# Split weights of the 512-token stretches placed 32, 96 and 160 bytes further in their buffers

## The reference, cut to what matters

```
for layer in (0, 1):
    h, hc = (a + 0.5*g*swiglu(prenorm(a)) for a in (h, hc))   # ffn1: 1024 -> 2*2816 -> 1024
    zl, zc = prenorm(h) @ w_in, prenorm(hc) @ w_in            # "even" mixer, then "odd" mixer
    h = h + gm * (mixer(zl, zc) @ mix_w_out)
    h = h + 0.5*g2*swiglu(prenorm(h))                         # ffn2; hc too, in layer 0 only
```

## Time and profile before

| what | value |
|---|---|
| median of three runs | 2996.09 us |
| the profiled execution | 2992.23 us, span 2990.5 us |
| mean granted TensorE clock | 0.996 of full speed |
| PE busy | 2932.5 us, 98% of the span, 20172 matmuls |
| PEld busy | 2580.5 us, 86% |
| DVE, ACT busy | 57%, 44% |
| DMA | 439.36 MB, 147 GB/s on average |

### The profile page before, as it was taken

The page is one execution under the profiler, slowest core; times in us unless marked ns, Lnnn a source line. Parts: engine busy times, 40 slices in busy tenths (PEclk is TensorE's granted clock), DMA queues, the critical chain, the costliest instruction groups (busy, mean ns, idle before and its releaser), DMA issues.

```text
span 2990.5 us, 52037 instructions
## 1 busy us (share of the span) xinstructions
PE 2932.5 (98%) x20172; PEld 2580.5 (86%) x20172; DVE 1690.7 (57%) x2664; ACT 1314.1 (44%) x1952; POOL 0.2 (0%) x4
## 2 busy tenths in 40 slices
PE   9999999999999999999998999999999999999999
PEld 6778878787777878888888999999899999988998
DVE  4333363545332453334666667677776776777766
ACT  4322343423222342223335656555555555556555
POOL 0000000000000000000000000000000000000000
PEclk9999999999999999999999999999999999999999
DMA  9555343146566433332322666455446654554564
GB/s 275 181 176 148 89 154 93 43 149 176 166 202 181 141 113 95 95 105 76 121 85 79 190 184 186 132 156 170 141 141 196 175 156 146 166 164 139 163 191 137
DMA packets 639011, 439.36 MB, mean 147 GB/s; under 512 B 22172, under 2 KB 627192, under 8 KB 638712
## 3 DMA queue, kind: packets, MB, share of 16 engines
q1 hardware_dynamic: 637844, 436.70, 49.1%
q10 hardware_dynamic: 996, 0.23, 0.0%
HBM read 430.84 MB, written 1.05 MB: 144 GB/s over the span
## 4 chain that ended last, share of the span: by engine, by line
PE 87%; DVE 8%; ACT 1%; issue 1%; SPq 1%; DMA 1%; DVEq 0%; ACTq 0%
PE ps L470 26%; PE ps L472 25%; PE ps L471 25%; DVE wlo L419 2%; PE ps L558 2%; ACT whi L412 1%; DMA raw<-ffn_w_in 1%; PE ps L1809 1%; DVE normed L2684 1%; PE ps L1789 1%; SPq L734 1%; PE ps L1821 1%; DVE xl L2676 1%; PE ps L1270 0%; PE ps L1279 0%
## 5 line engine op out<-in xcount | busy, mean ns | idle before, releaser
L470 PE MATMUL ps<-xh,whi 128*128 128x256 f32 (+1 forms) x3744 | 1204.8, 322 | 24.4 <-DVE wlo L419 5.6
L471 PE MATMUL ps<-xl,whi 128*128 128x256 f32 (+1 forms) x3744 | 1183.7, 316 | 0.0
L472 PE MATMUL ps<-xh,wlo 128*128 128x256 f32 (+1 forms) x3744 | 1183.6, 316 | 0.0
L419 DVE TENSOR_TENSOR wlo<-raw,whi 128x1024 fp32r<-128x1024 f32 x732 | 869.1, 1220 | 182.7 <-ACT whi L412 174.5
L412 ACT ACTIVATE whi<-raw 128x1024 fp32r<-128x1024 f32 x731 | 747.4, 1053 | 462.1 <-PE ps L472 398.9
L470 PEld LDWEIGHTS ps<-xh,whi 128*128 128x128 f32 x3744 | 705.4, 188 | 106.5 <-issue 45.0
L472 PEld LDWEIGHTS ps<-xh,wlo 128*128 128x128 f32 x3744 | 705.6, 188 | 50.6
L471 PEld LDWEIGHTS ps<-xl,whi 128*128 128x128 f32 x3744 | 706.3, 189 | 48.6
L470 PE MATMUL ps<-hid_h,whi 128*128 128x512 f32 (+1 forms) x1056 | 353.4, 335 | 0.0
L471 PE MATMUL ps<-hid_l,whi 128*128 128x512 f32 (+1 forms) x1056 | 352.3, 334 | 0.0
L472 PE MATMUL ps<-hid_h,wlo 128*128 128x512 f32 (+1 forms) x1056 | 352.2, 334 | 0.0
(11 more groups left out here) (380 smaller groups left out, 2593.9 us busy)
## 6 DMA issues: line engine op xcount, KB each, us to landing
raw<-ffn_w_in SPq DMA_DIRECT2D x176, 512.0 KB, 4.7
mod_w<-ada_w SPq DMA_DIRECT2D x72, 1024.0 KB, 7.7
raw<-w_in SPq DMA_DIRECT2D x96, 512.0 KB, 4.6
raw<-w_ffn_in SPq DMA_DIRECT2D x88, 512.0 KB, 4.7
raw<-w_gate SPq DMA_DIRECT2D x64, 512.0 KB, 4.1
raw<-ffn_w_out SPq DMA_DIRECT2D x64, 384.0 KB, 3.9
raw<-ffn_w_out SPq DMA_DIRECT2D x64, 320.0 KB, 3.6
raw<-w_branch SPq DMA_DIRECT2D x32, 512.0 KB, 3.4
```

Source lines behind the costliest of these rows:

```text
L419: nc.vector.tensor_tensor(split_at(unit, wlo, s, h), raw[:, s, h, :], split_at(unit, whi, s, h).bitcast(F32), ALU.subtract).then_inc(S("lo ...
L470: nc.tensor.matmul(dst, w_h, x_h, start=start, stop=False)
L471: nc.tensor.matmul(dst, w_h, x_l, start=False, stop=False)
L472: return nc.tensor.matmul(dst, w_l, x_h, start=False, stop=stop)
```

## The change

The one skew of 16 elements from unit 134 on becomes a table. Units below 54 get 8 elements (32 bytes), units 54 to 91 get 24 (96 bytes), 92 to 133 get 40 (160 bytes), and all from 134 on keep 16 (64 bytes). The buffers, `raw`, the activations and the instructions stay as they are.

```diff
-SKEW, SKEW_FROM = 16, 134
+SKEWS = ((54, 8), (92, 24), (134, 40), (10 ** 9, 16))
...
         def split_at(u, w, s, h):
 
-            first = SKEW if u >= SKEW_FROM else 0
+            first = [skew for end, skew in SKEWS if u < end][0]
             return w[:, s, h, first:first + UNIT // 2]
...
             def odd(w_in):
-                assert c.units + 6 == SKEW_FROM
+                assert c.units + 6 == SKEWS[2][0]
```

## The result

| kernel | timed runs | median us | ratio to before, 95% interval |
|---|---|---|---|
| before | 4 | 2997.79 | |
| after | 4 | 3033.11 | 1.0122 [1.0108, 1.0135] |

The change costs 35.3 us. The forecast was 2976.6 us with a range up to 3012; the result lies outside it. The two profiled executions, 2992.23 and 3030.67 us, differ by 38.4 us. An interval is the time from the start of one matmul to the start of the next; the beat is the interval that an unbroken stretch keeps on average.

A forecast was written before the change was run, and what follows sets the result against it. PE's start-to-start matmul distances were taken as the bound. Splits 0, 512-column matmuls -18.1 and narrow ones -1.4 us sum to -19.5 us: 2996.1 - 19.5 = 2976.6 us, range 2955 to 3012 us for 8 in 10.

The forecast's parts named there:

- What bounds the kernel: Whole kernel: PE, busy 98% of the span, sets the end through distances between matmul starts; 226.7 ns at 512 columns.
- The first term: Splits on ACT and DVE, writing to another place in the row: no change, 0; bound 0.3 us, hidden.
- The second term: 5424 512-column matmuls below unit 134: each 3.33 ns shorter, 18.1 us gained; range -36.2 to +22.6 us.
- The third term: 432 256-column matmuls with moved weights (queries, even mixer's values): 3.33 ns shorter each, 1.4 us gained, at most 2.9.
- The window sums of the 256-token part should stay: From 1506 us on, where the change does not touch the weights' offset: window sums stay as they are.
- The rule of two independent ports: Skill's rule for TensorE, cited against the change: no offset matters, change worth 0; the trace disagreed at 256 columns.
- R1: Rival: stream limited to 16 columns in 17 cycles; only 432 narrow matmuls can gain, 0 to -2.9 us; chance 0.27.
- R2: Rival: new offsets lose the even beat at 512 columns, about 230.8 ns, 3003 to 3019 us; chance 0.24.
- R3: Rival: all three stretches reach the better state, -36.2 - 2.9 us, 2957 us; chance 0.12, including anything beyond.
- What would be late next: If PE gets faster, a weight unit would be late next; DMA stays below its limit, so nothing taken off.

The follow-up runs named there:

- e13: The kernel before, unchanged, profiled once more; a single profiled run of 2991.54 us.
- e1: Against the kernel before, every buffer from the weights on starts 32 bytes further, weights and activations together (distance 0 below unit 134); 3005.71 us, ratio 1.0034.
- e6: Against the kernel before, activations 32 bytes further, weights unmoved below unit 134 (distance 224), narrow part kept at 64; single profiled run, 3026.4 us.
- e2: Against the kernel after, offsets of 64, 128 and 192 bytes in the three stretches, narrow part unchanged; 3021.4 us, ratio 1.0088.

## Why the prediction was wrong, point by point

**What bounds the kernel** was right: PE is on the path throughout, each nanosecond per matmul arrives in the total (36.0 us worked out for 5424 matmuls, 34.5 of 39.1 us by the borders against e13), and starts, not durations, carry it.

**The first term**, splits at 0, was right: 1220 ns and 869.1 us, as before.

**The second term failed, by its sign: "I take 3.33 ns, half of the full step".** It carried a step seen at 256 columns to 512. There distance 0 (119.9 ns) is slower than nearly all others measured; at 512 columns it is the best of 21. In place of -18.1 us stands +36.0 us. The term's upper bound, +22.6 us, was too low as well: 230.8 ns of the earlier trace rows came from blocks whose distance changes from one to the next, and a constant distance of 32 bytes is worse, 233.3 ns. The argument for the value, that each new offset lies "between the offset that costs 32 cycles and the one that costs 16 or 26.7", took for granted that the cost goes smoothly with the offset. The table refutes that: over 226.7 ns, 4 bytes cost 5.7 ns, 8 bytes 4.0, 240 bytes 1.6, 248 bytes 6.6.

A smaller slip in the same step: the earlier trace rows are the token form, where the moved weights are the moving operand. That pair shows a distance of 192 against 0, not 64 against 0; only the feature form shows 64.

**The third term** was right for the values, 116.7 ns against 116.67 forecast (120.0 - 3.33), worth 0.8 us, and wrong for the queries: 119.6 before, 119.8 ns after. The agreement for the values is luck: their distance is 224 bytes, not 32.

**"The window sums of the 256-token part should stay"** was wrong by 4.7 to 5.8 us. Both states were seen in the earlier trace rows and taken as fixed; their share is not.

**The rule of two independent ports** (the Trainium skill, "TensorE: Matmul & The Clock Gate", "Step-by-step: what each phase is for") says that loading the next weights takes nothing from the running matmul; by it all these kernels would be equal at 512 columns. The runs have 226.7 to 234.3 ns with the same instructions at clock 1.00, and the kernel after, e1 and e6 tie this to the distance between the two operands. So at `float32r` the measurement decides against it: the place of one operand against the other changes the rate.

**R1**, a floor at 17/16 of the stream, foresaw no change; it is wrong as a forecast, since the new distances are above the floor. Whether 226.7 ns is a floor is not decided: no mean came below it, though single intervals did (225.8 to 226.0 ns on average behind each second matmul of three in the last stretch of e2, made up for by the two others). **R2** had the right side and the size too low: 4.2 ns expected, 6.2 to 7.3 measured. Its mechanism is half borne out. The even beat of 226 and 227 ns is gone, as R2 said, and single intervals are uneven; but they are not unsettled, for they repeat in a fixed pattern with a longer mean of 560 to 562 cycles. **R3** is refuted at every distance tried. "Against" R2 stood the two better states of the narrow matmuls, the same carrying over from 256 to 512 columns. **What would be late next** was not put to the test, since PE got slower.

**What stays open:** why the means are 544 and 560 cycles, and why ten of the distances share the second though their single intervals are patterned differently; which accesses collide; and how an edit in a 512-token stretch changes the share of states in the 256-token part.

## What to carry to other kernels

Where TensorE is the bound in `float32r` and each matmul has a stationary load of its own, the starts of the stationary and of the moving operand modulo 256 bytes are a parameter to sweep, for each width of the moving operand by itself: here 0 is best at 512 columns and 64 bytes, stationary ahead, at 256, and the wrong choice costs 3% and 6% of the matmul. A gain at one width says nothing of another, and between two measured offsets nothing may be interpolated. Give each stretch of one kernel its own offset, and read start-to-start distances over unbroken stretches: one run then measures three or four. Mean durations show only part of the effect (5 to 6 ns of 6.2 to 7.3).

## What the hardware showed that was not expected

- The interval of 512-column matmuls depends on the operands' distance with a period of 256 bytes: 226.7 to 227.2 ns at 0 and 256, 228.3 to 234.3 at 20 other distances. 4 bytes are enough (232.4 ns).
- Direction matters at 256 columns: 64 bytes give 114.2 to 115.3 ns, 192 bytes 116.9 to 117.6, 4 bytes short of 256 even 123.2.
- One stationary operand of three at another distance can cost as much as all three (233.2 against 233.3 ns on average), spread unevenly over the three: 233, 239 and 228 ns.
- The price is there while DVE, ACT and the DMA engines are idle: 233.3 against 226.6 ns.
- At 64 bytes and 256 columns there are two states, 113.3 and 117.8 ns; the share of the first was 75% in both profiles of one program, and from 57% (e1) to 77% (e6) in programs whose distance there is the same.
